# The end of a recurrent (mLSTM) layer, ordered by heads: first projection slab ahead of the last two heads' transposes

## What is computed

```python
# mlstm_layer, cut: 4 heads of 256 value columns
ht = mlstm_chunkwise(q, k, v, i_pre, log_sigmoid(f_pre))   # sum of decayed q.k weights times v, over max(|den|, exp(-m))
ht = sigmoid(o) * ht
ht = rms_norm(ht, hnorm_g)                                  # per head, over its 256 columns
y = ht * silu(z)
return y @ w_out                                            # 1024 x 1024, then added to the residual
```

## Time and profile before

| | us |
|---|---|
| runs of the kernel | 1701.69, 1706.86, 1709.94 (median 1706.86) |
| the profiled execution, its own time | 1701.95 |
| span from its first to its last instruction | 1700.2 |
| PE busy (matmul records) | 1577.0, 93% of the span |
| mean granted TensorE clock | 0.975 of full |

### The profile page before, as it was taken

How to read it: one execution, slowest core, us unless ns; L and a number is a source line. 1 busy time by engine, 2 the same in 40 slices (tenths; PEclk the granted TensorE clock), 3 DMA queues, 4 the chain that set the end, 5 groups by cost and what they waited for, 6 DMA issues and landing times.

```text
span 1700.2 us, 19463 instructions
## 1 busy us (share of the span) xinstructions
PE 1577.0 (93%) x7449; PEld 1277.2 (75%) x7449; DVE 754.3 (44%) x1217; ACT 598.6 (35%) x885; POOL 685.6 (40%) x264
## 2 busy tenths in 40 slices
PE   4999999899999997999999997899978979998798
PEld 4876876766888876888887886788757768776577
DVE  2155955262332316666662006620162455464743
ACT  4244245463223324222221125222342434455442
POOL 4331465222555544444444443444312443445432
PEclk9999999999999998999999998999999989999999
DMA  5311412101333332333332223243302231322021
GB/s 195 113 60 62 137 59 60 38 0 53 93 93 100 116 100 63 98 99 99 99 99 99 91 60 76 74 108 91 111 1 70 80 95 55 110 77 75 1 70 54
DMA packets 145412, 137.42 MB, mean 81 GB/s; under 512 B 8721, under 2 KB 119185, under 8 KB 145341
## 3 DMA queue, kind: packets, MB, share of 16 engines
q1 hardware_dynamic: 141860, 131.09, 26.0%
q10 hardware_dynamic: 3480, 5.36, 0.9%
HBM read 134.31 MB, written 2.12 MB: 80 GB/s over the span
## 4 chain that ended last, share of the span: by engine, by line
PE 83%; DVE 6%; issue 5%; POOL 3%; ACT 3%; SPq 0%; DMA 0%; POOLq 0%; ACTq 0%; DVEq 0%
PE banks L638 80%; POOL w_lo L516 2%; PE banks L658 2%; PE banks L785 1%; ACT w_hi L1183 1%; DVE resid L1865 1%; DVE xs L1663 1%; DVE prob L2068 1%; DVE o L1977 1%; POOL rstd L544 0%; DVE rows_out L1857 0%; DVE prob L1677 0%; DMA vec_rows<-in_hnorm_a 0%; ACT stick_a L1368 0%; ACT stick_a L1369 0%
## 5 line engine op out<-in xcount | busy, mean ns | idle before, releaser
L516 POOL TENSOR_TENSOR w_lo<-raw,w_hi 128x2048 fp32r<-128x2048 f32 x122 | 562.8, 4614 | 780.7 <-ACT w_hi L1183 776.2
L638 PE MATMUL banks<-h_hi,w_hi 128*128 128x512 f32 x856 | 341.6, 399 | 5.2 <-POOL w_lo L516 2.4
L638 PE MATMUL banks<-h_hi,w_lo 128*128 128x512 f32 x856 | 334.9, 391 | 0.0
L638 PE MATMUL banks<-h_lo,w_hi 128*128 128x512 f32 x856 | 334.4, 391 | 0.0
L1183 ACT ACTIVATE w_hi<-raw 128x2048 fp32r<-128x2048 f32 x126 | 240.6, 1909 | 238.8 <-PE banks L638 232.8
L638 PE MATMUL banks<-w_hi,h_hi 128*128 128x512 f32 (+1 forms) x608 | 225.0, 370 | 5.2 <-POOL w_lo L516 2.5
L638 PE MATMUL banks<-w_hi,h_lo 128*128 128x512 f32 (+1 forms) x608 | 223.1, 367 | 0.0
L638 PE MATMUL banks<-w_lo,h_hi 128*128 128x512 f32 (+1 forms) x608 | 223.0, 367 | 0.0
L638 PEld LDWEIGHTS banks<-h_hi,w_hi 128*128 128x128 f32 x856 | 161.9, 189 | 41.5 <-issue 5.2
L638 PEld LDWEIGHTS banks<-h_hi,w_lo 128*128 128x128 f32 x856 | 161.2, 188 | 34.3
L638 PEld LDWEIGHTS banks<-h_lo,w_hi 128*128 128x128 f32 x856 | 161.7, 189 | 31.6
(11 more groups left out here) (291 smaller groups left out, 2303.0 us busy)
## 6 DMA issues: line engine op xcount, KB each, us to landing
raw<-in_w_in SPq DMA_DIRECT2D x56, 512.0 KB, 4.1
raw<-in_w_ffn_in SPq DMA_DIRECT2D x44, 512.0 KB, 4.6
raw<-in_w_in_a SPq DMA_DIRECT2D x32, 512.0 KB, 5.4
raw<-in_w_ffn_out SPq DMA_DIRECT2D x22, 512.0 KB, 3.9
raw<-in_w_ple_gate SPq DMA_DIRECT2D x16, 512.0 KB, 4.5
raw<-in_w_in_b SPq DMA_DIRECT2D x16, 512.0 KB, 4.3
raw<-in_w_mem_kv SPq DMA_DIRECT2D x8, 512.0 KB, 5.0
raw<-in_w_out SPq DMA_DIRECT2D x8, 512.0 KB, 3.6
```

The costliest lines, as they stand in the source:

```text
L516: pool.tensor_tensor(slot_of(w_lo, slot), slot_of(raw, slot), slot_of(w_hi, slot).bitcast(F32), ALU.subtract).then_inc(lo_made, 1)
L638: return pe.matmul(out, lhsT, rhs, start=start, stop=stop, **kw)
```

## The change

The names y2 and y2b now stand for the first and the last four column tiles of y. The transposes of y2 go to banks 0 to 3 and those of y2b to banks 6, 7, 4, 5. Of p0 and y, the order by which the counters run is k 0 to 3, p0, k 4 to 7.

- PE: the wait for `em_col` (`m_cols`) moves from ahead of head 0 to ahead of its output products. At step 4, k 0 and 1 are transposed ahead of head 3's output products, k 2 and 3 behind them; then the projection's first slab runs. Between its first and second slab PE waits for `m_h` 16, and transposes p0 and k 4 to 7.
- ACT: slab `wout2`+1 is split into its high part behind head 0's `decay`. The high parts of k 0 and 1 come behind the squares of head 2, those of k 2 and 3 behind the squares of head 3, then p0, then k 4 to 7.
- POOL: the low part of slab `wout2`+1 is made in four quarters, one behind each head's causal selects (and its root, where there is one).
- DVE: a head's mean square comes behind `wts` and ahead of the outputs of the next head; y of that head comes behind those outputs, as before. At step 4 the low parts of k 0 and 1 stand ahead of head 3's outputs, those of k 2 and 3 behind them; p0 and k 4 to 7 come behind y of head 3.
- `y2_lo` lies at another place in SBUF, over `decay0`, `wts0` and the gate rows, and no longer over `v1`.

```diff
@@ -71,13 +71,21 @@
 SLABS = _number_stages()
...
-TRANSPOSES = [("vec", 0), ("mem", KD), ("x", KD), ("ffn", KD), ("a2", KD), ("p0", 2), ("y2", KD), ("g0", KD),
+TRANSPOSES = [("vec", 0), ("mem", KD), ("x", KD), ("ffn", KD), ("a2", KD), ("y2", 4), ("p0", 2), ("y2b", 4), ("g0", KD),
               ("kv3", KD), ("b3", KD), ("p1", 2), ("g1", KD)]
...
     _n += _k
+TR["y2b"] -= 4
+
+def transposed_bank(name, k):
+    return {"y2": k, "p0": 4 + k, "y2b": 4 + (k - 2) % 4}.get(name, 4 + (TR[name] + k) % 4)
 NORMS = {n: i for i, n in enumerate(["mem", "x", "post", "ffn", "fpost", "a2", "g0", "kv3", "g1"])}
@@ -303,7 +311,7 @@
     wts = [arena("wts0", 70, PACK), place("wts1", 85, PACK)]
...
     i_row, f_row, nf_row, a_row, m_row, em_row = rows4
-    y2_hi, y2_lo = arena("y2_hi", 0, KD * S, F32R), arena("y2_lo", 16, KD * S, F32R)
+    y2_hi, y2_lo = arena("y2_hi", 0, KD * S, F32R), arena("y2_lo", 65, KD * S, F32R)
     ple_proj, ple_gate = arena("ple_proj", 33, ROW), arena("ple_gate", 49, ROW)
...
     pT_hi, pT_lo = place("pT_hi", 68, 2 * S, F32R), place("pT_lo", 72, 2 * S, F32R)
@@ -598,9 +606,10 @@
             keep_causal(decay[h % 2], m_em, False)
...
                 head_root(h - 2)
+            lo_quarter(BASE["wout2"] + 1, h)
         head_root(2)
         head_root(3)
-        split_lo(BASE["wout2"] + 1, BASE["pp0"] + 1)
+        split_lo(BASE["wout2"] + 2, BASE["pp0"] + 1)
         root("g0")
...
         root("kv3")
@@ -650,12 +659,12 @@
                 n = TR[name] + k
...
                     pe.wait_ge(t_lo, n - 3)
-                if name == "y2":
+                if name in ("y2", "y2b"):
                     pe.wait_ge(m_y, k // 2 + 1)
...
                         pe.wait_ge(n_xs, scaled + t + 1)
-                    ins = pe.transpose(banks[:, 4 + n % 4, t * P:(t + 1) * P], rows(t)[:, k * P:(k + 1) * P], const("ident"))
+                    ins = pe.transpose(banks[:, transposed_bank(name, k), t * P:(t + 1) * P], rows(t)[:, k * P:(k + 1) * P], const("ident"))
                 ins.then_inc(t_done, 1)
...
         def wait_slab(stage, i, s, j, unroll=2):
@@ -1027,7 +1036,6 @@
         ins.then_inc(m_colT, 1)
...
         pe.wait_ge(ev_v, EV_V["wout2"])
-        pe.wait_ge(m_cols, 2)
         pe.wait_ge(ld_late, 48)
...
             if step < 4:
@@ -1043,8 +1051,11 @@
                 ins.then_inc(m_s, 1)
...
                 h = step - 1
+                if step == 1:
+                    pe.wait_ge(m_cols, 2)
                 if step == 4:
                     pe.wait_ge(m_w, 4)
+                    transposes("y2", rows_of(o2), 2)
                 for t in range(NT):
...
                         pe.wait_ge(m_h, 4 * (h - 1) + t + 1)
@@ -1052,10 +1063,16 @@
                         off = TILE_AT[kt] + (t - kt) * P
...
                     ins.then_inc(m_out, 1)
-        pe.wait_ge(m_h, 16)
-        pe.wait_ge(ld_p, 16)
-        transposes("p0", lambda t: p_rows[:, t * 256:(t + 1) * 256], 2)
-        gemm_wide("wout2", 0, y2_hi, y2_lo, 0, ready=transposed_ahead("y2", rows_of(o2)))
+        transposes("y2", rows_of(o2), 2, first=2)
+        def rest_of_y2():
+            pe.wait_ge(m_h, 16)
+            pe.wait_ge(ld_p, 16)
+            transposes("p0", lambda t: p_rows[:, t * 256:(t + 1) * 256], 2)
+            transposes("y2b", rows_of(o2), 4, first=4)
+        gemm_wide("wout2", 0, y2_hi, y2_lo, 0, ready=lambda k: pe.wait_ge(t_lo, TR["y2" if k < 4 else "y2b"] + k + 1), between=rest_of_y2)
         gemm_wide("wout2", 1, y2_hi, y2_lo, 1)
...
         def gated_addition(g_name, gate_stage, plain_stage, p_hi, p_lo):
@@ -1261,7 +1278,7 @@
                 n = TR[name] + k
...
                 scale = 1.0 if gain is None else col[:, gain + k:gain + k + 1]
-                act.activation(dst[:, k * tok:(k + 1) * tok], banks[:, 4 + n % 4, 0:tok], ACT.Copy, scale=scale).then_inc(t_hi, 1)
+                act.activation(dst[:, k * tok:(k + 1) * tok], banks[:, transposed_bank(name, k), 0:tok], ACT.Copy, scale=scale).then_inc(t_hi, 1)
@@ -1479,6 +1496,8 @@
                     ins = act.activation(decay[h % 2][:, TILE_AT[kt]:TILE_AT[kt] + TILE_N[kt]], banks[:, 3, kt * P:], ACT.Exp,
...
                 ins.then_inc(m_e, 1)
+                if step == 0:
+                    split_hi(0, "wout2", 0)
             if step >= 2:
...
                 if h:
@@ -1488,10 +1507,11 @@
                     ins = act.activation(junk[:, 256 * t:256 * t + 256], o2[:, t * D + h * 256:t * D + (h + 1) * 256], ACT.Square,
...
                 ins.then_inc(m_ss, 1)
+            if step >= 4:
+                transposed_hi("y2", 2 * step - 6, V_HEAD, y2_hi, first=2 * step - 8)
         act.wait_ge(m_ss, 4)
         transposed_hi("p0", 2, None, pT_hi)
-        split_hi(0, "wout2", 0)
-        transposed_hi("y2", KD, V_HEAD, y2_hi)
+        transposed_hi("y2b", KD, V_HEAD, y2_hi, first=4)
...
             for c in range(2):
@@ -1667,7 +1687,7 @@
                 n = TR[name] + k
...
                 scale = 1.0 if gain is None else col[:, gain + k:gain + k + 1]
-                dve.scalar_tensor_tensor(out=lo[:, k * tok:(k + 1) * tok], in0=banks[:, 4 + n % 4, 0:tok], scalar=scale,
+                dve.scalar_tensor_tensor(out=lo[:, k * tok:(k + 1) * tok], in0=banks[:, transposed_bank(name, k), 0:tok], scalar=scale,
                                          in1=hi[:, k * tok:(k + 1) * tok].bitcast(F32), op0=ALU.mult, op1=ALU.subtract).then_inc(t_lo, 1)
...
         def normalise(u, buf, n):
@@ -1953,6 +1973,13 @@
                 if h >= 2:
...
                 dve.tensor_tensor(wts[h % 2][:], flat[:, 0:PACK], decay[h % 2][:], ALU.mult).then_inc(m_w, 1)
+            if step >= 2:
+                h = step - 2
+                dve.wait_ge(m_ss, h + 1)
+                c = slice(4 * h, 4 * h + 4)
+                dve.tensor_scalar(head_ms[:, c], head_ss[:, c], 1.0 / 256, EPS, ALU.mult, ALU.add).then_inc(m_ms, 1)
+            if step == 4:
+                transposed_lo("y2", 2, V_HEAD, y2_hi, y2_lo)
             if 1 <= step <= 4:
...
                 for t in range(NT):
@@ -1965,19 +1992,18 @@
                     link(dve.reciprocal(den_inv[:, i4], den[:, i4]))
...
                                              op1=ALU.mult).then_inc(m_h, 1)
-                if h == 3:
-                    transposed_lo("p0", 2, None, pT_hi, pT_lo)
-            for h in ([step - 2] if 2 <= step <= 4 else [3] if step == 5 else []):
-                dve.wait_ge(m_ss, h + 1)
-                c = slice(4 * h, 4 * h + 4)
-                dve.tensor_scalar(head_ms[:, c], head_ss[:, c], 1.0 / 256, EPS, ALU.mult, ALU.add).then_inc(m_ms, 1)
+            if step == 4:
+                transposed_lo("y2", 4, V_HEAD, y2_hi, y2_lo, first=2)
+            if step >= 2:
+                h = step - 2
                 dve.wait_ge(m_rs, h + 1)
...
                 ins.then_inc(m_y, 1)
-        transposed_lo("y2", KD, V_HEAD, y2_hi, y2_lo)
+        transposed_lo("p0", 2, None, pT_hi, pT_lo)
+        transposed_lo("y2b", KD, V_HEAD, y2_hi, y2_lo, first=4)
...
             for c in range(2):

```

## The result

The changed kernel took 1694.3 us (median of four runs, 1690.85 to 1696.06) beside 1708.4 us for the kernel before in the same comparison (1701.69 to 1710.21): ratio 0.9934, 95% interval 0.9911 to 0.9957, which is 11.3 us less; the two medians by themselves lie 14.1 apart. Measured a second time the ratio was 0.9927 (0.9905 to 0.9949). The forecast was 12.9 us less, at 1693.

A forecast was written before the change was run, and what follows sets the result against it. PE holds 83% of the chain, but DVE carries it late in the head loop, with y of head 3 held by POOL. The steps move the mark from 1305.6 to 1292.7, 12.9 us less: 1693 forecast, range 1685 to 1702.

The forecast's parts named there:

- Step 1, start: PE without the em_col wait ahead of head 0: everything to head 2's outputs moves 1.0 us earlier.
- Step 2, quarters: POOL's four quarters of slab wout2+1, 5.2 us instead of 4.50: cost 0, no DVE operation held.
- Step 3, mean square ahead: DVE's y of head 0 no longer waits 1.14 us for the root; wts of head 3 starts at 1252.0, against 1253.62.
- Steps 4 and 5: DVE's head 3 outputs end at 1265.2, against 1266.27; low parts of k 2 and 3 at 1267.2 and 1267.9.
- Step 6, first slab: PE waits 3.8 us for k 2; eight products at low clock charged about 1.6 us, bounds 0 and 1.7; ends 1278.4.
- Step 7, cover: First slab covers DVE's y of heads 2 and 3; the 4.23 us hold goes; wout2+2 is ready 2.7 us early.
- Step 8, between the slabs: PE's fill from 1278.4 to first product at 1281.7, second slab to 1292.7; up to 1.7 us more if clock falls.
- the clock one: Clock stays up in head 0's logits and the slab's products: 15.9 us gained, 1690; chance 0.13.
- quarters holding DVE: POOL's quarters hold DVE, price 5.2 us: 7.7 us gained, 1699; chance 0.11.
- the longer fill: Fill between the slabs is a new stall, or ACT's wout2+2 copy comes late: 10 us gained, 1696; chance 0.11.
- half clock through both slabs: PE stays at half clock through both slabs, 0.2 us more per product: 4.6 us slower, 1711; chance 0.02.
- does not do what it says: First slab still waits for y of head 3, 5 us come back: 8 us gained, 1699; chance 0.02.

The follow-up runs named there:

- e3: Changed kernel with POOL's low part of slab wout2+1 made whole again, behind the roots of heads 2 and 3; stretch 69.30 us (changed kernel 67.10).
- e5: Changed kernel with 14 extra products filling PE's gap between k 1 and k 2 of the first slab; stretch 66.57 us.
- e7: Changed kernel with k 0 to 3 made ahead of head 3's outputs and the later transposes inside the first slab; stretch 61.65 us, ratio 0.9884.
- e2: Kernel before with only PE's wait for em_col moved to ahead of head 0's output products; stretch 80.34 us (before 80.40).
- e1: Kernel before with only slab wout2+1 split early, POOL's low part in quarters behind each head; stretch 79.34 us (before 80.40).
- e9: Changed kernel with DVE's mean squares put back behind the outputs of the next head; stretch 73.01 us.
- changed, again: Changed kernel run once more with no edit; stretch 65.53 us, against 67.10 in its first execution.
- e6: Changed kernel with all four column tiles, k 0 to 3, made ready ahead of head 3's outputs; stretch 63.14 us, ratio 0.9898.

## Why the prediction was right, step by step

The sign, the size and the mechanism held: 12.9 us forecast, 13.3 and 14.9 in the stretch, 11.3 by the ratio. Counted from wts of head 2, so without the start, the forecast had the mark at 48.8 (1292.7 - 1243.9), and it was at 49.85 and 48.28. That the first execution came within 0.4 us of the sum is partly luck: the start gave 1.4 more than forecast, the rest 1.0 less, and both come mainly from the clock. With the slow start that e3, e5 and four other kernels with the moved wait had, the changed kernel would gain 10.9 to 12.5 us by an estimate from the table.

- *Step 1, start*, failed. The pick did start 0.96 us earlier, but "all of it moves by -1.0" happened in no execution: 2.4 where the clock stayed up, 0.03 where it fell, 0.7 in e7. I had kept the clock's low stretch in its place; e2 shows that it moves along and takes the gain back.
- *Step 2, quarters*: cost 0 was right, L1975 and the reciprocals were not held. So was the refusal to take the page's rule ("GPSIMD Engine Reference" of the Trainium skill, Key points) to cover one-source reciprocals: 16 of them lie within 0.166 us here. For two SBUF inputs the trace agrees with that rule (2.97, 2.66 and 5.99 us instead of 1.67). The prediction let y fall outside the quarters "by the times below", and it did; it had not said that this hangs on step 3, without which the quarters hold y by 1.0 us twice (e1, e9).
- *Step 3, mean square ahead*: wts 3 came 7.94 us after wts 2, against 8.1 forecast and 8.73 before.
- *Steps 4 and 5*: head 3's outputs ended 20.8 after wts 2 (forecast 21.3), and k 2 could start at 22.7 (23.3).
- *Step 6, first slab*: the gap came (3.51 us). The term for the low clock was mis-sized: eight slow products, 1.6 us, were charged, and about 15 and 6 were measured. The 42 products from k 2 on took 12.58 and 10.98 us, and 9.65 at full clock in e5, so the term was 2.9 and 1.3. Its upper bound, 1.7 us, came from one row, the restart at 1280.
- *Step 7, cover*: right; e3 takes away the early split and the 4.3 us stay hidden. ACT's copy of slab wout2+2 began at 1288.20, its low part was ready 4 us ahead of need.
- *Step 8, between the slabs*: 3.3 us to the first product (1284.26 to 1287.58), as forecast, then 11.2 instead of 11.0. The clock did not fall a second time.
- *From one execution to the median*: 1693 against 1694.3 fits, but unchanged code moved a single execution by 6.5 us, half the gain.

Of the rivals, the clock one came in by halves (start up, slab low); quarters holding DVE (not here, but in e1 and e9 they do), the longer fill, half clock through both slabs and "does not do what it says" are excluded by the rows above.

## What to carry to other kernels

When the next stage's first part needs only the first half of a loop's results, put everything it needs, transposes, copies and low parts, ahead of the loop's last iteration on every engine, not only on the one that computes: here the copies left behind head 3 on ACT and DVE cost a gap and then a slow restart, 4.8 and 6.4 us more (changed, again and first, against e6). A slice of work for a second engine was free here only where no DVE instruction with both inputs in SBUF followed the same release; look at what the releaser of one wait releases besides. And judge such a change by the stretch between two marks in the trace, since the total carries what the clock did in unchanged code.

## What the runs showed of the hardware that I had not expected

- The same code up to a point ran at two rates: the logits of heads 0 and 1 at 2.42 us, or 3.29 and 3.90 (e2), or 2.42 and 4.11 (e7), after the same 0.87 us of idle time. Starting PE earlier did not shorten a low stretch, only moved it (e2).
- After the same 3.5 us gap the low stretch lasted for 6 products in one execution and for 14 or 15 in another, 2.7 and 6.2 us.
- An operation of DVE with both inputs in SBUF is not slowed by POOL's subtraction but held to its end: 5.99 us for four beside 4.58 of POOL, 2.97 and 2.66 beside 1.27 (the first with the causal selects behind it), 1.67 alone. In before, e1 and e3 one of the four takes the whole delay and ends 0.27 or 0.28 us behind POOL's instruction. Beside the causal selects none is held: two of the four take 0.62 instead of 0.47 us (e1).
- Between two executions, unchanged code of some 1225 us differed by 6.5 us, with granted clocks of 1.00 and 0.98 in its windows. In the clock records of the two traces PE was granted half clock for 47.8 us of it in the kernel before and for 58.0 in the changed one. By an estimate from these, 10.2 us more at half clock cost up to 5.1 of the 6.5.
